# Feed-forward and expert layers: where TensorE transposes the hidden tiles, set further apart

## The chip, the cores and the metric

The kernel runs on one core of a Trainium2 chip. The metric is the device time of one execution in microseconds (us); lower is better. TensorE (PE in the profile) multiplies, VectorE (DVE) and ScalarE (ACT) read its results out of PSUM, GpSimd (POOL) helps in the first layer, SyncE (SP) issues the weight loads.

## What is computed

Two layers over 640 tokens (128 context tokens and 512 latent ones), model width 1024. Each layer has a token mixer and then a channel mixer; the change touches the channel mixers alone: a dense SwiGLU in layer 0, a top-2-of-8 expert SwiGLU in layer 1.

```python
def swiglu(h, w_gu, w_down):
    gate, up = jnp.split(h @ w_gu, 2, axis=-1)
    return (jax.nn.silu(gate) * up) @ w_down

def moe_swiglu(h, router_w, w_gu, w_down):          # D_FF_E = 1408, N_EXPERTS = 8
    probs = jax.nn.softmax((h @ router_w).astype(jnp.float32), axis=-1)
    top_p, top_i = lax.top_k(probs, TOP_K)
    ...
    for e in range(N_EXPERTS):
        y = y + gates[..., e:e + 1] * swiglu(h, w_gu[e], w_down[e])
    return y
```

The dense layer has `D_FF = 2816`, which the kernel computes as two "experts" of 1408 over all tokens.

## The kernel before

**Tiles.** Tokens go in tiles of 128. The dense layer runs its two passes over 5 tiles each. In the expert layer each expert takes its own tokens, gathered into `n` tiles, a number known only at run time; in this case the eight experts have 1, 2, 2, 1, 2, 1, 2 and 3 tiles, 14 in all.

**Precision.** Every float32 product is made of three matmuls of split operands: `hi*whi`, `lo*whi`, `hi*wlo` (lines 1261 to 1263, into one PSUM bank). `whi` is written by ScalarE (line 1988, one instruction for each half slot), `wlo` by VectorE (lines 2652 and 2661; in the dense layer every odd one by GpSimd, line 1505).

**Half slots.** Weights come in 18 slots for an expert, each of two half slots `m` of two rows of 128 (one row in two places). Gate and up take six column groups `j = 0..5` of four half slots `s = 0..3`; a group is 512 columns wide, but the last, `j = 5`, only 256. Down takes two groups of six half slots (`m = 24..35`). In each half slot (`half`, line 1247) TensorE goes over all token tiles, 6 matmuls for a tile. Four half slots of `whi` and `wlo` exist, so ScalarE splits `m + 4` once `m` has been used (`high_after`, line 1988). The SBUF ring `wring` holds three slots; SP refills one when both of its halves are split (line 504).

**The hidden tiles.** When a column group is done, ScalarE takes silu of the gate half into `hbuf` (line 2043) and VectorE multiplies the up half in (line 2686, signal `h_done`). TensorE then transposes tile `t` of `hbuf` (`h_group`, lines 1229 to 1235: two 128x128 transposes, one for `j = 5`), all into the same PSUM bank 7. ScalarE copies it to `hTh` (line 2032), VectorE writes the rest, `hTl` (line 2674, signal `hTl_ready`). Since there is one bank, `h_group` of a tile waits at line 1232 until the `hTl` of the tile before is written. So the transposes of a column group form a chain PE, ACT, DVE, PE, tile by tile.

**Where they stand.** The transposes of group `j - 1` are issued in the second half slot (`s = 1`) of group `j`, that of tile `t` right behind the matmuls of tile `t` (`after`, lines 1329 and 1330); those of `j = 5` stand in the same way in half slot 1 of the down product (line 1350). In the expert layer each further tile sits in a nested `If` on `n` (`nest`, line 1237).

**What sets the order.** Each engine's program is written out by hand and runs in order. On ScalarE it is, for each `j`: `high_after(4j)`, then `h_high` (a loop over the `n` tiles that waits for each tile's transposes), `high_after(4j+1)`, `high_after(4j+2)`, the silus, `high_after(4j+3)`. VectorE: `low` of the half slot 4j+4, `h_low` over the `n` tiles, `odd_low` (4j+5), `low` (4j+6), products, `odd_low` (4j+7). At the end of `j = 1` of an expert ScalarE also issues the loads of the next expert's tokens (line 2019), one for each tile, ahead of the splits of `j = 2`.

Of the kernel before, what the change touches and what calls it, by code (L numbers as in the profile page):

```python
# [151 lines left out]
def backbone(nc, A, out_prompt, out_sample, out_state, mod_dram, xs_dram, ys_dram, xpark, combo_dram):  # L152
    with ExitStack() as ctx:
# [565 lines left out]
        def _(pe):  # L719
# [29 lines left out]
            for k in range(KD):  # L749
                s = slot(k)  # L750
# [465 lines left out]
            def ffn(l):  # L1216
# [12 lines left out]
                def h_group(q, j, t):  # L1229

                    pe.wait_ge(f["h_done"], q + 1)
                    pe.wait_ge(f["hTl_ready"], q + 1)
                    for c in range(2 if j < 5 else 1):
                        mm = pe.transpose(bank(7)[:, c * P:(c + 1) * P], hbuf[:, t, c * P:(c + 1) * P], ident)  # L1234
                    mm.then_inc(f["hT_ps"], 1)

                def nest(n, body, t=0):

                    body(t)
                    if t + 1 < T:  # L1240
                        if isinstance(n, int):
                            nest(n, body, t + 1)
                        else:
                            with pe.If(n > t + 1):
                                nest(n, body, t + 1)

                def half(e, m, n, hi, lo, c0, bk, first, last, done, width, free, after=None):

                    k, s = m // 2, m % 2
                    nk = half_rows(k, s)  # L1250
                    pe.wait_ge(slot_split[s], split_count(k, e, l))
                    hs = (2 * ring0 + m) % HALVES

                    def tile(t):
                        if first:
                            free(t)
                        tt = slice(t * P, (t + 1) * P)
                        for c in range(nk):
                            wh, wl = whi[:, hs, c, 0:width], wlo[:, hs, c, 0:width]
                            out = bank(bk(t))[:, 0:width]  # L1260
                            pe.matmul(out, hi[:, c0 + c, tt], wh, start=(first and c == 0), stop=False)  # L1261
                            pe.matmul(out, lo[:, c0 + c, tt], wh, start=False, stop=False)  # L1262
                            mm = pe.matmul(out, hi[:, c0 + c, tt], wl, start=False, stop=(last and c == nk - 1))  # L1263
                        mm.then_inc(done if last else f["half_done"], 1)
                        if after is not None:
                            after(t)
                    nest(n, tile)
# [36 lines left out]
                def expert(e, n, c):  # L1304

                    n2 = T
                    if l:
                        pe.wait_ge(f["xTl_ready"], (c + n) * 2 + 1)
                    for j in range(6):
                        bk = (lambda t, j=j: t if j % 2 == 0 or t > 1 else 5 + t)  # L1310
                        def free(t, j=j):
                            if l == 0 and c == 0 and j == 0:
                                pe.wait_ge(f["xTl_ready"], 2 * (t + 1) + 1)
                            if t < 2 and j < 2:


                                if j:
                                    pe.wait_ge(f["y_copied"], c * 2 + 1)
                            elif j == 0 and l == 0:
                                pe.wait_ge(f["y_copied"], c + t + 2 if c else 1)  # L1320
                            elif j == 0:
                                pe.wait_ge(f["y_copied"], c * 2 + 1)
                            else:
                                pe.wait_ge(f["h_done"], c * 6 + n * (j - 1 if t > 1 else j - 2) + (t + 1))
                        for s in range(4):
                            after = None
                            if l == 0 and e == 0 and j == 0 and s == 0:
                                after = lambda t: h_columns(T - 2 + t) if t < 2 else None
                            if s == 1 and j:
                                after = lambda t, j=j: h_group(c * 6 + n * (j - 1) + t, j - 1, t)  # L1330
                            half(e, 4 * j + s, n, xTh, xTl, 2 * s, bk, s == 0, s == 3, f["gu_ps"],
                                 512 if j < 5 else 256, free, after)
                            if l and j == 1 and s == 0:
                                n2 = next_count(pe, e)

                    if l:
                        pe.wait_ge(f["xs_in"], (c + n + n2) * 16)
                    for a in range(2):
                        bk = (lambda t, a=a: t if a == 0 or t > 1 else 5 + t)
                        free = (lambda t: pe.wait_ge(f["y_copied"], c * 2 + (t + 2))) if a else \  # L1340
                            (lambda t: pe.wait_ge(f["h_done"], c * 6 + n * 5 + (t + 1)) if t > 1 else None)
                        for s in range(6):
                            m = 6 * a + s
                            if l == 0 and e and m >= 9:
                                if m == 9:
                                    last_halves((33, 34, 35), bk, f["down_ps"])
                                continue
                            if a == 0 and s == 0:
                                pe.wait_ge(f["hTl_ready"], c * 6 + n * 5 + 1)
                            after = (lambda t: h_group(c * 6 + n * 5 + t, 5, t)) if m == 1 else None  # L1350
                            half(e, 24 + m, n, hTh, hTl, 2 * s, bk, s == 0, s == 5, f["down_ps"], 512,
                                 free if a == 0 else (lambda t: free(t) if t > 1 else None), after)
                            if m == (3 if l else 2):

                                pe.wait_ge(f["hTl_ready"], c * 6 + n * 6 + 1)
                            if m == 4 and l:

                                pe.wait_ge(f["xTl_ready"], 2 * (c + n) + 2)
                            if m == 11:

                                pe.wait_ge(f["y_copied"], c * 2 + n + 1)
                            if m >= 2 and l:
                                t2, g = (m - 2) // 2, m % 2
                                if t2 == 0:
                                    xs_group(c + n, t2, g, xs_bank(m), 1)
                                else:
                                    with pe.If(n2 > t2):
                                        xs_group(c + n, t2, g, xs_bank(m), 1 if m == 4 else 0)
                    return n2
# [1655 lines left out]
```

## Time and profile before

| | us |
|---|---|
| median of 3 runs | 2067.35 |
| lowest, highest | 2066.21, 2075.73 |
| span of the profiled execution | 2066.3 |
| TensorE busy in it | 1925.3 (93%) |
| VectorE busy | 1120.1 (54%) |
| ScalarE busy | 749.5 (36%) |
| waits of the `hbuf` transposes for `hTl` | 13.6, in 16 places |

The profiled execution lies 1.05 us under the median. The feed-forward layer stands from about 740 to 1200 us of the span, the experts from about 1282 to 2017 us. "Busy" of TensorE is the time in which a matmul is in flight; matmuls overlap, so small delays between them don't show as idle time. They are read from the starts: in these stretches a 512-column matmul starts 0.227 us after the one before, a 256-column one 0.118 us after.

### The profile page before, as it was taken

To read this page: it belongs to the slowest core of one execution; us is meant where nothing else is said; L and a number is where in the kernel's file an instruction comes from. 1 tells how busy PE (TensorE), PEld (TensorE's weight loads), DVE (VectorE), ACT (ScalarE), POOL (GpSimd) and SP (SyncE) were. 2 spreads that over 40 slices of the span, in tenths; PEclk is the share of its full clock that TensorE was granted. 3 is DMA by queue.
4 is the path that set the end of the run, shared out by engine and by line. 5 is a ranking of instruction groups with operands and counts; after the bars stand their busy time and mean duration, and the time that the engine had idled before them with its cause. 6 is when DMAs were issued, how large, how long until landed. Compare 5 with 4: busy or idle time off the path is not lost. (4 is left out here: it accounts for less than half of the span.)

```text
span 2066.3 us, 39450 instructions
## 1 busy us (share of the span) xinstructions
PE 1925.3 (93%) x14595; PEld 1556.4 (75%) x14596; DVE 1120.1 (54%) x1756; ACT 749.5 (36%) x1292; POOL 407.6 (20%) x316
## 2 busy tenths in 40 slices
PE   5899999999999999999999997899998998899994
PEld 3888888888875487887888776777776786777781
DVE  3566777677674734232222385754558457554337
ACT  2523442443231122221222113744457447443332
POOL 0244344434421222121121333000000000000003
PEclk7899999999999999999999999999999999999997
DMA  8143234224326342243323506966569569654354
GB/s 298 32 146 97 91 116 137 80 93 141 116 77 213 109 143 78 93 152 99 98 92 105 174 21 246 312 216 193 181 211 317 190 198 328 217 176 164 101 174 168
DMA packets 186858, 320.03 MB, mean 155 GB/s; under 512 B 26137, under 2 KB 77729, under 8 KB 186619
## 3 DMA queue, kind: packets, MB, share of 16 engines
q1 hardware_dynamic: 170683, 286.00, 42.2%
q10 hardware_dynamic: 12192, 17.00, 2.4%
q0 software_dynamic: 3744, 13.63, 1.8%
q8 instruction: 175, 2.87, 0.6%
q14 instruction: 64, 0.52, 0.1%
HBM read 283.89 MB, written 32.67 MB: 153 GB/s over the span
## 5 line engine op out<-in xcount | busy, mean ns | idle before, releaser
L1261 PE MATMUL pp<-whi,xTh 128*128 128x512 f32 (+1 forms) x1152 | 445.5, 387 | 23.9 <-issue 8.8
L1988 ACT ACTIVATE whi<-wring 128x1024 fp32r<-128x1024 f32 (+1 forms) x324 | 314.7, 979 | 410.7 <-PE pp L1263 353.9
L1263 PE MATMUL pp<-wlo,xTh 128*128 128x512 f32 (+1 forms) x1152 | 432.4, 375 | 0.0
L1262 PE MATMUL pp<-whi,xTl 128*128 128x512 f32 (+1 forms) x1152 | 431.7, 375 | 0.0
L2652 DVE TENSOR_TENSOR wlo<-wring,whi 128x1024 fp32r<-128x1024 f32 (+1 forms) x180 | 209.6, 1164 | 269.8 <-ACT whi L1988 221.8
L1261 PEld LDWEIGHTS pp<-whi,xTh 128*128 128x128 f32 x1152 | 219.1, 190 | 74.0 <-issue 28.7
L1263 PEld LDWEIGHTS pp<-wlo,xTh 128*128 128x128 f32 x1152 | 218.8, 190 | 39.2
L1262 PEld LDWEIGHTS pp<-whi,xTl 128*128 128x128 f32 x1152 | 219.6, 191 | 34.6
L1261 PE MATMUL pp<-whi,hTh 128*128 128x512 f32 x503 | 202.3, 402 | 7.7 <-DVE ybuf L2604 2.3
L1263 PE MATMUL pp<-wlo,hTh 128*128 128x512 f32 x503 | 196.5, 391 | 0.0
L1262 PE MATMUL pp<-whi,hTl 128*128 128x512 f32 x503 | 196.1, 390 | 0.0
L2661 DVE TENSOR_TENSOR wlo<-wring,whi 128x1024 fp32r<-128x1024 f32 (+1 forms) x144 | 159.1, 1105 | 65.8 <-ACT whi L1988 55.1
L1505 POOL TENSOR_TENSOR wlo<-wring,whi 128x1024 fp32r<-128x1024 f32 (+1 forms) x38 | 97.4, 2565 | 373.7 <-ACT whi L1988 348.5
L1675 POOL DMA_INDIRECT yA<-expert_out,pos x5 | 4.7, 947 | 746.4 <-POOLq L1671 745.2
L2674 DVE TENSOR_TENSOR hTl<-pp,hTh 128x256 f32 (+1 forms) x144 | 57.7, 401 | 165.3 <-ACT hTh L2032 165.3
L2686 DVE TENSOR_TENSOR hbuf<-hbuf,pp 128x256 f32<-128x256 f32 (+1 forms) x144 | 56.6, 397 | 145.6 <-ACT hbuf L2043 145.6
L1543 POOL TENSOR_TENSOR x<-x,cmd 128x320 f32<-128x320 f32 x96 | 94.7, 1004 | 183.0 <-DVE x L2311 96.9
L1838 ACT ACTIVATE x<-pp 128x320 f32<-128x320 f32 (+1 forms) x96 | 37.6, 435 | 232.2 <-PE pp L914 232.0
L1261 PEld LDWEIGHTS pp<-whi,hTh 128*128 128x128 f32 x503 | 94.5, 188 | 31.8 <-DVE ybuf L2604 4.5
L1263 PEld LDWEIGHTS pp<-wlo,hTh 128*128 128x128 f32 x503 | 94.4, 188 | 20.5
L1262 PEld LDWEIGHTS pp<-whi,hTl 128*128 128x128 f32 x503 | 94.7, 188 | 17.5
L2032 ACT ACTIVATE hTh<-pp 128x256 f32 (+1 forms) x144 | 52.6, 365 | 137.8 <-PE pp L1234 137.7
(331 smaller groups left out, 3128.6 us busy)
## 6 DMA issues: line engine op xcount, KB each, us to landing
wring<-in_moe_w_gu SPq DMA_DIRECT2D x320, 256.0 KB, 3.8
wring<-in_ada_w SPq DMA_DIRECT2D x80, 512.0 KB, 4.7
wring<-in_moe_w_down SPq DMA_DIRECT2D x160, 256.0 KB, 3.7
wring<-in_ffn_w_gu SPq DMA_DIRECT2D x80, 256.0 KB, 3.0
wring<-in_dn_w_in SPq DMA_DIRECT2D x128, 128.0 KB, 2.7
wring<-in_ffn_w_down SPq DMA_DIRECT2D x40, 256.0 KB, 3.0
expert_in<-zeros SPq DMA_DIRECT2D x36, 256.0 KB, 3.3
wring<-in_ada_w SPq DMA_DIRECT2D x32, 256.0 KB, 5.5
```

The costliest lines, as they stand in the source:

```text
L1261: pe.matmul(out, hi[:, c0 + c, tt], wh, start=(first and c == 0), stop=False)
L1262: pe.matmul(out, lo[:, c0 + c, tt], wh, start=False, stop=False)
L1263: mm = pe.matmul(out, hi[:, c0 + c, tt], wl, start=False, stop=(last and c == nk - 1))
L1505: pool.tensor_tensor(wlo[:, hs, 0:nk, 0:w], wring[:, ring_p.slot(k), 2:2 + nk, 0:w], whi[:, hs, 0:nk, 0:w].bitcast(F32), ALU.subtract).the ...
L1543: pool.tensor_tensor(per_block(offd[:, d, :]), per_block(adiag[:, d, :]), diag_bc(LEVEL + lv, d), ALU.mult)\
L1838: act.activation(vt[rows_of, d, :], PP[d][rows_of, 0:NC], ACT.Copy).then_inc(S["vt_sb"], 1)
L1988: act.activation(whi[:, hs, 0:nk, 0:w], wring[:, ring_v.slot(k), 2 * s:2 * s + nk, 0:w], ACT.Copy)\
L2032: act.activation(hTh[:, 2 * j:2 * j + nk, bass.ds(t * P, P)], bank(7)[:, 0:nk * P].rearrange("p (k t) -> p k t", k=nk), ACT.Copy)\
L2652: dve.tensor_tensor(wlo[:, hs, :, 0:w], wring[:, ring_v.slot(k), 0:2, 0:w], whi[:, hs, :, 0:w].bitcast(F32), ALU.subtract).then_inc(slot_s ...
L2661: dve.tensor_tensor(wlo[:, hs, 0:nk, 0:w], wring[:, ring_v.slot(k), 2:2 + nk, 0:w], whi[:, hs, 0:nk, 0:w].bitcast(F32), ALU.subtract).then ...
L2674: dve.tensor_tensor(hTl[:, 2 * j:2 * j + nk, bass.ds(t * P, P)], bank(7)[:, 0:nk * P].rearrange("p (k t) -> p k t", k=nk), hTh[:, 2 * j:2 ...
L2686: dve.tensor_tensor(hbuf[:, t, 0:w], hbuf[:, t, 0:w], bank(b)[:, w:2 * w], ALU.mult)\
```

## The change

Only the places of `h_group` in TensorE's program move. `half` gets a second hook, `ahead(t)`, called ahead of tile `t`'s matmuls; `after(t)` stays behind them.

- Dense layer, `j = 5` (256 columns): the transposes stand behind tiles 0, 2 and 4 of half slot 1 and behind tiles 1 and 3 of half slot 2, two tiles' matmuls apart instead of one. The other groups of the dense layer are as they were.
- Experts, every group and the down product: tile 0's transposes stay behind tile 0 in half slot 1; those of tile `t >= 1` stand ahead of tile `t`'s matmuls in half slot 2. An expert with one tile is as it was.

```diff
+                def h_groups(q0, j, s, short):
+
+                    def group(t):
+                        h_group(q0 + t, j, t)
+                    if l:
+                        return (lambda t: group(t) if t == 0 else None) if s == 1 else None, \
+                            (lambda t: group(t) if t else None) if s == 2 else None
+                    if short:
+                        return lambda t: group(t // 2 if s == 1 else 3 + t // 2) if t % 2 == s - 1 else None, None
+                    return group if s == 1 else None, None
+
...
-                def half(e, m, n, hi, lo, c0, bk, first, last, done, width, free, after=None):
+                def half(e, m, n, hi, lo, c0, bk, first, last, done, width, free, after=None, ahead=None):
...
+                        if ahead is not None:
+                            ahead(t)
...
-                            if s == 1 and j:
-                                after = lambda t, j=j: h_group(c * 6 + n * (j - 1) + t, j - 1, t)
+                            ahead = None
+                            if s in (1, 2) and j:
+                                after, ahead = h_groups(c * 6 + n * (j - 1), j - 1, s, j == 5)
...
-                            after = (lambda t: h_group(c * 6 + n * 5 + t, 5, t)) if m == 1 else None
+                            after, ahead = h_groups(c * 6 + n * 5, 5, m, False) if m in (1, 2) else (None, None)
```

TensorE's program, dense layer, first pass, `j = 5`, half slot 1, from tile 0's transposes to tile 1's. `hTl_ready0` and `h_done0` are the dense layer's signals. Before:

```order
L1234 MATMUL pp<-cm,hbuf 128x128 [waits hTl_ready0,h_done0]
L1234 MATMUL pp<-cm,hbuf 128x128
L1261 MATMUL pp<-whi,xTh 128x256
L1262 MATMUL pp<-whi,xTl 128x256
L1263 MATMUL pp<-wlo,xTh 128x256
L1261 MATMUL pp<-whi,xTh 128x256
L1262 MATMUL pp<-whi,xTl 128x256
L1263 MATMUL pp<-wlo,xTh 128x256
L1234 MATMUL pp<-cm,hbuf 128x128 [waits hTl_ready0,h_done0]
```

Now, from tile 2's transposes, which end half slot 1, on to where tile 3's stand in half slot 2 (the product's lines are 1274 to 1276 here):

```order
L1234 MATMUL pp<-cm,hbuf 128x128 [waits hTl_ready0,h_done0]
L1234 MATMUL pp<-cm,hbuf 128x128
L1274 MATMUL pp<-whi,xTh 128x256 [waits slot_split_first]
L1275 MATMUL pp<-whi,xTl 128x256
L1276 MATMUL pp<-wlo,xTh 128x256
...
L1276 MATMUL pp<-wlo,xTh 128x256
L1234 MATMUL pp<-cm,hbuf 128x128 [waits hTl_ready0,h_done0]
```

Between two transposes with their waits there were 6 matmuls; there are 12 now.

TensorE's program, expert layer, `j = 1`: `slot_split_first` is the wait with which a half slot begins, the branches are the nested `If`s. Before, in half slot 1, tile 0's transposes, tile 1's matmuls, tile 1's transposes:

```order
L1231 ISA
L1234 MATMUL pp<-cm,hbuf 128x128 [waits hTl_ready1,h_done1]
L1234 MATMUL pp<-cm,hbuf 128x128
L1244 COMPARE_AND_BRANCH
L1261 MATMUL pp<-whi,xTh 128x512
L1262 MATMUL pp<-whi,xTl 128x512
L1263 MATMUL pp<-wlo,xTh 128x512
L1261 MATMUL pp<-whi,xTh 128x512
L1262 MATMUL pp<-whi,xTl 128x512
L1263 MATMUL pp<-wlo,xTh 128x512
L1231 REGISTER_ALU
L1234 MATMUL pp<-cm,hbuf 128x128 [waits hTl_ready1,h_done1]
```

Now, the start of half slot 2, where tile 1's transposes stand:

```order
L1255 UNCONDITIONAL_BRANCH
L1262 REGISTER_ALU
L1274 MATMUL pp<-whi,xTh 128x512 [waits slot_split_first]
L1275 MATMUL pp<-whi,xTl 128x512
L1276 MATMUL pp<-wlo,xTh 128x512
L1274 MATMUL pp<-whi,xTh 128x512
L1275 MATMUL pp<-whi,xTl 128x512
L1276 MATMUL pp<-wlo,xTh 128x512
L1255 COMPARE_AND_BRANCH
L1231 REGISTER_ALU
L1234 MATMUL pp<-cm,hbuf 128x128 [waits hTl_ready1,h_done1]
L1234 MATMUL pp<-cm,hbuf 128x128
```

Tile 1's transposes have moved from the end of half slot 1, behind one tile's matmuls, to behind tile 0 of half slot 2: with two tiles they stand 12 matmuls behind tile 0's transposes instead of 6, and no longer right ahead of a change of half slot. The programs of the other engines are unchanged.

## Rows read from the trace of the kernel before

**Rows 1.** The page: shares of the chain that ended last, by engine.

```profile
PE 28%; DVE 3%; issue 2%; DMA 2%; ACT 2%; SPq 1%; ACTq 0%; another core or an unknown queue 0%; DVEq 0%; POOL 0%; POOLq 0%
```

**Rows 2.** What the transposes of `hbuf` (line 1234) waited for: us, times.

```profile
  DVE hTl L2674: 13.6, 16
```

**Rows 3.** Timeline, dense layer, j = 5: start, duration, engine, line [idle before].

```profile
870.45 0.41 PE L1234 MATMUL pp<-cm,hbuf 128*128 128x128 f32 x2 [0.55 <-DVE hTl L2674]
...
872.12 0.41 PE L1234 MATMUL pp<-cm,hbuf 128*128 128x128 f32 x2 [0.55 <-DVE hTl L2674]
```

**Rows 4.** Timelines of ScalarE and VectorE over the same tile.

```profile
870.99 0.38 ACT L2032 ACTIVATE hTh<-pp 128x256 f32 x1 [1.29 <-PE pp L1234]
...
871.55 0.42 DVE L2674 TENSOR_TENSOR hTl<-pp,hTh 128x256 f32 x1 [1.25 <-ACT hTh L2032]
```

**Rows 5.** Timeline of TensorE, dense layer, j = 4 (512 columns), two tiles' transposes.

```profile
845.58 0.41 PE L1234 MATMUL pp<-cm,hbuf 128*128 128x128 f32 x2
...
847.25 0.41 PE L1234 MATMUL pp<-cm,hbuf 128*128 128x128 f32 x2
```

**Rows 6.** Timelines of TensorE, third expert (two tiles), 512 columns wide.

```profile
1459.64 0.40 PE L1263 MATMUL pp<-wlo,xTh 128*128 128x512 f32 x1
...
1460.65 0.39 PE L1262 MATMUL pp<-whi,xTl 128*128 128x512 f32 x1
...
1481.53 0.39 PE L1263 MATMUL pp<-wlo,xTh 128*128 128x512 f32 x1
...
1482.21 0.39 PE L1262 MATMUL pp<-whi,xTl 128*128 128x512 f32 x1
...
1486.55 0.39 PE L1263 MATMUL pp<-wlo,xTh 128*128 128x512 f32 x1
1486.78 0.39 PE L1261 MATMUL pp<-whi,xTh 128*128 128x512 f32 x1
...
1514.79 0.40 PE L1263 MATMUL pp<-wlo,hTh 128*128 128x512 f32 x1
...
1515.75 0.39 PE L1262 MATMUL pp<-whi,hTl 128*128 128x512 f32 x1
```

**Rows 7.** The same expert, j = 5 (256 columns), timeline of TensorE.

```profile
1503.56 0.38 PE L1234 MATMUL pp<-cm,hbuf 128*128 128x128 f32 x2
...
1504.37 0.28 PE L1263 MATMUL pp<-wlo,xTh 128*128 128x256 f32 x1
1505.92 0.41 PE L1234 MATMUL pp<-cm,hbuf 128*128 128x128 f32 x2 [1.26 <-DVE hTl L2674]
...
1506.66 0.28 PE L1262 MATMUL pp<-whi,xTl 128*128 128x256 f32 x1
```

**Rows 8.** Timeline of TensorE, seventh expert (two tiles), j = 2.

```profile
1791.15 0.38 PE L1234 MATMUL pp<-cm,hbuf 128*128 128x128 f32 x2
...
1794.71 0.41 PE L1234 MATMUL pp<-cm,hbuf 128*128 128x128 f32 x2 [1.79 <-DVE hTl L2674]
```

**Rows 9.** Timeline of TensorE, last expert (three tiles), j = 5.

```profile
1960.40 0.41 PE L1234 MATMUL pp<-cm,hbuf 128*128 128x128 f32 x2 [1.27 <-DVE hTl L2674]
...
1962.07 0.66 PE L1234 MATMUL pp<-cm,hbuf 128*128 128x128 f32 x2 [0.55 <-DVE hTl L2674]
```

**Rows 10.** Windows: length, busy (count) of PE, PEld, DVE, ACT, POOL; clock; DMA share; GB/s.

```profile
1453.00:1533.00 80.00, 77.18 (x367) 62.61 (x368) 44.88 (x58) 39.74 (x59) 0.00 (x0) 1.00 0.60 189
1535.00:1592.00 57.00, 50.29 (x234) 38.76 (x233) 42.93 (x49) 38.37 (x52) 0.00 (x0) 1.00 0.91 311
...
1960.00:1965.00 5.00, 4.05 (x22) 3.77 (x23) 1.83 (x4) 1.76 (x3) 0.00 (x0) 0.70 0.39 128
```

**Rows 11.** Timeline of VectorE, third expert: the split behind `j = 3`'s transposes.

```profile
1485.37 1.22 DVE L2661 TENSOR_TENSOR wlo<-wring,whi 128x1024 fp32r<-128x1024 f32 x1 [0.45 <-ACT whi L1988]
```

**Rows 12.** The chain that ended last, in the fourth expert (one tile).

```profile
1545.35 1.07 ACT whi L1988
...
1556.16 8.60 DMA wring<-in_moe_w_gu
```

More of the change, by code:

```diff
@@ L1328, in expert @@
                                 after = lambda t: h_columns(T - 2 + t) if t < 2 else None
-                            if s == 1 and j:
-                                after = lambda t, j=j: h_group(c * 6 + n * (j - 1) + t, j - 1, t)
+                            ahead = None
+                            if s in (1, 2) and j:
+                                after, ahead = h_groups(c * 6 + n * (j - 1), j - 1, s, j == 5)
                             half(e, 4 * j + s, n, xTh, xTl, 2 * s, bk, s == 0, s == 3, f["gu_ps"],
-                                 512 if j < 5 else 256, free, after)
+                                 512 if j < 5 else 256, free, after, ahead)
                             if l and j == 1 and s == 0:
@@ L1349, in expert @@
                                 pe.wait_ge(f["hTl_ready"], c * 6 + n * 5 + 1)
-                            after = (lambda t: h_group(c * 6 + n * 5 + t, 5, t)) if m == 1 else None
+                            after, ahead = h_groups(c * 6 + n * 5, 5, m, False) if m in (1, 2) else (None, None)
                             half(e, 24 + m, n, hTh, hTl, 2 * s, bk, s == 0, s == 5, f["down_ps"], 512,
-                                 free if a == 0 else (lambda t: free(t) if t > 1 else None), after)
+                                 free if a == 0 else (lambda t: free(t) if t > 1 else None), after, ahead)
                             if m == (3 if l else 2):
```

## Prediction

> **What bounds the kernel now.** I read the page first: by the table above TensorE is busy for 93% of the span, ScalarE for 36% and VectorE for 54%, and TensorE holds by far the largest named share of the chain that ended last [rows 1]. So the question is where TensorE loses time at the instructions that the change moves. The view of what line 1234 waits for gives it: 13.6 us in 16 places, all for `hTl` [rows 2]. The timelines place them: 4 in each pass of the dense layer at 0.55 us (4.4) [rows 3], one in each of the four two-tile experts at `j = 5` at 1.26 us (5.0) [rows 7], two in the last expert, 1.27 and 0.55 us (1.8) [rows 9], one of 1.79 us in the seventh expert [rows 8], and what remains of the 13.6, 0.6 us, in the second expert at `j = 2`.
>
> What ends these waits is the chain through bank 7. From the start of a tile's transposes at 870.45, ScalarE starts 0.54 us later and takes 0.38, VectorE starts at 1.10 and ends at 1.52 [rows 4], and the next transposes start at 1.67 us [rows 3]. With 512 columns the same spacing stands in the trace, 1.67 us, but without idle time [rows 5]: one tile's 6 matmuls (1.36 us) and the transposes' own time fill it. With 256 columns 6 matmuls are only 0.71 us.
>
> Idle time is not all. I take as the cost of a group of transposes the time from the last matmul ahead of it to the second one behind it, less two matmuls. Tile 0's group, for which nothing has to be waited, costs 1482.21 - 1481.53 - 0.45 = 0.23 us; tile 1's, at the end of the half slot, costs 1460.65 - 1459.64 - 0.45 = 0.55 us at `j = 1` and 1515.75 - 1514.79 - 0.45 = 0.51 us in the down product [rows 6]. Of the five such places in a two-tile expert these are the first and the last; the three between them cost 0.60, 0.67 and 0.74. A change of half slot without transposes costs nothing: 1486.55 to 1486.78 is one matmul [rows 6]. So the extra arises where TensorE's sequencer has just been held by the wait for `hTl` and then has the branches of the nested `If` and the next half slot's wait ahead of it with nothing queued.
>
> **Dense layer, j = 5.** Two tiles of 256 columns (12 x 0.118 = 1.42 us) and a group's 0.23 make 1.65 us between transposes, against the 1.67 us that the chain needs. The transposes keep their spacing, but each of the four gaps in a pass now holds one tile's matmuls more, 0.71 us: 8 x 0.71 = **5.7 us**. The first and the last transposes keep their times, so ScalarE and VectorE, which run in order behind them, are no later on the clock; only TensorE is earlier, by 2.8 us a pass. The next thing that could be late is the split of half slot 24. It follows the last `hTl` and ends some 2.7 us after the last transposes start (1.10 + 0.42 + 1.22, a split's time from rows 11), and TensorE needs it after one more tile and one half slot of 256 columns (6 x 0.71 = 4.2 us). Cover is 1.5 us, so I cost it at nothing; were the split 2.8 us later than read, a pass would give back 1.3 us.
>
> **Two-tile experts, 512 columns and down.** Tile 1's transposes now stand 12 matmuls behind tile 0's: 0.23 + 12 x 0.227 = 2.95 us, against 1.67 us for the chain. The wait is over 1.3 us before TensorE gets there, so the sequencer stays ahead, and the group should cost what tile 0's costs. The five places cost 0.55 + 0.60 + 0.67 + 0.74 + 0.51 = 3.07 us, and would cost 4 x 0.23 + 0.12 = 1.04 (the down group has one transpose, 0.12 for tile 0): 2.03 us for an expert, four experts **8.1 us**. At the least the end-of-half part stays, at the most the groups cost as said.
>
> **Two odd places.** In the seventh expert ScalarE is still busy with the token loads, and the chain takes 3.56 us [rows 8]; with 2.95 us of cover 0.6 of the 1.79 us wait stays: 1.1 us more than the ordinary place, and 0.75 at the 0.6 us wait of the second expert: **1.9 us**.
>
> **Two-tile experts, j = 5.** VectorE splits a half slot first, so the chain takes 2.36 us; cost now 1506.66 - 1504.37 - 0.24 = 2.05 us [rows 7]. Matmuls cover 0.23 + 12 x 0.118 = 1.65 us; 0.71 us of wait stays, and the group, behind a wait again, costs 0.31 on top (1.67 - 1.36, rows 5). That would save 1.03. Behind it only one 0.71 us tile stands ahead of the next change of half slot, and I charge 0.25 us for it (0.55 - 0.31): 0.8 us, four times **3.2 us**; between 2.2 (the wait alone) and 4.1.
>
> **Last expert.** Three tiles: tile 1's group gets three tiles of cover, tile 2's keeps one. At 512 columns tile 2's end-of-half cost goes (0.3 at each of four places), tile 1's 0.06 each, down 0.3; at `j = 5` the wait of 1.27 us goes with its group's slack (1.45), the second, 0.55 us, stays but moves off the half slot's end (0.4): **3.6 us**. There the clock also fell: behind these two waits the window of 5 us shows a mean granted clock of 0.70 [rows 10], that is 3 us at 1.2 instead of 2.4 GHz, which costs 1.5 us. With the first wait gone I take **1.3 us** of it as saved; it could be none.
>
> **Sum.** 5.7 + 8.1 + 1.9 + 3.2 + 3.6 + 1.3 = 23.8 us off a span of 2066.3: 2042.5. The profiled execution lies 1.05 us under the median, so 2043.6 for the median. What no edit touches: one-tile experts, three of eight.
>
> **Rival 1: the end-of-half cost stays (2051.3).** If the 0.3 us is the price of the half slot's change beside any group, or comes back in half slot 2, only the waits go. Lost are 0.24 + 0.29 + 0.36 + 0.43 + 0.3 = 1.6 us in four experts and 1.2 in the last, 7.7 us. Against it: changes of half slot without transposes cost nothing [rows 6]. The Trainium skill (Advanced Engine Details and Errata, section Control Flow Timing) puts a compare-and-branch at about 108 ns; by that 21 places would give 2.3 of the 7.7 us and the time would be about 2049. The trace shows more than that for one place, and the rows decide for me.
>
> **Rival 2: given back in the one-tile experts (2053).** There the DMA engines are busy for 0.91 of the time at 311 GB/s, against 0.60 and 189 GB/s with two tiles [rows 10], and the chain runs through an 8.6 us load [rows 12]. If weights set the clock of the whole stretch, the gains of the second, third and fifth experts, about 9.5 us, end as longer waits in the fourth and sixth. Against it: the load starts when a ring slot is free, and the chain leads from it back to a ScalarE split at 1545.35 that waited for TensorE [rows 12]. A TensorE that comes earlier frees it earlier.
>
> **Rival 3: slower (2078).** ScalarE runs in order. In `h_high` it now waits for tile 1's transposes a tile longer (1.36 us), and behind that wait stand the splits of half slots 4j+5 and 4j+6, on VectorE their `wlo`, on SP the loads into the slots that these free. If TensorE had to wait for them, 25 places at up to 1.4 us would cost 35 us, 11 more than is saved. It decides once the slack of that split is under 1.4 us. In the third expert it ended at 1485.37 + 1.22 = 1486.6 [rows 11] and was needed 24 matmuls after 1486.78, at 1492.2: slack 5.6 us. The loads into the freed slots start up to 1.4 us later too; with the DMA engines busy for 0.60 of the time they have room [rows 10]. The Trainium skill (TensorE: Matmul & The Clock Gate, section on the array as 16x 32x32) says that ScalarE and VectorE are strict FIFO with 8 entries; by that rule the held splits can't pass the wait. No row here shows a split that passed one.
>
> **How the numbers follow.** Forecast 0.77 (own range 2040 to 2048: upper ends of the bounded terms above, down to the clock's gain lost, `j = 5` at its lower end and the dense cover partly gone), rival 1 0.10, rival 2 0.07, rival 3 0.04, the rest for what I don't see. The range 2040 to 2054 takes in the first two rivals. About 0.5% (10 us) is what a measurement of this kernel can tell from no change; the first three cases all lie beyond it. Faster 0.91, same 0.05, slower 0.04.
>
> **What would show it.** Right: the waits of line 1234 for `hTl` fall from 13.6 us to about 4.5 (four of 0.7, 0.6, 0.55 and little else); the dense `j = 5` transposes stay 1.67 us apart without idle; tile 1's group in experts costs 0.23 us; two-tile experts shorten by some 3 us each, one-tile experts stay. Wrong: waits of line 1274 for `wlo` in two-tile experts (rival 3), longer one-tile experts (rival 2), costs of 0.5 us at the change from half slot 1 to 2 or 2 to 3 (rival 1), or a clock that falls at another place.

## The result, and the profile after

| | before, beside it | changed |
|---|---|---|
| median of 4 runs, us | 2069.5 | 2044.72 |
| lowest to highest | 2066.21 to 2075.73 | 2039.09 to 2045.42 |
| span of the profiled execution | 2066.3 | 2043.6 |
| TensorE busy in it | 1925.3 | 1915.1 |

The ratio is 0.987, with a 95% interval of 0.9855 to 0.9886. The forecast was 2043.6 us, the stated range 2040 to 2054.

In the changed kernel line 1261 has become 1274 (`hi*whi`), 1262 is 1275, 1263 is 1276; `hTl` is written at line 2688, `hTh` at 2046, `hbuf` at 2057 and 2700, `whi` at 2002, `wlo` at 2666 and 2675. The transposes are still issued at line 1234. The view of what line 1234 waited for, of the changed kernel (us in total, times), answers to [rows 2]:

```profile
  DVE hTl L2688: 3.2, 6
```

The waits for `hTl` fell from 13.6 us in 16 places to 3.2 in 6; about 4.5 had been forecast.

**Dense layer, j = 5.** The timeline of TensorE (start us, us, engine, line, operation) at the same two groups as in [rows 3]:

```profile
869.86 0.28 PE L1276 MATMUL pp<-wlo,xTh 128*128 128x256 f32 x1
869.98 0.41 PE L1234 MATMUL pp<-cm,hbuf 128*128 128x128 f32 x2
...
871.54 0.28 PE L1276 MATMUL pp<-wlo,xTh 128*128 128x256 f32 x1
871.66 0.40 PE L1234 MATMUL pp<-cm,hbuf 128*128 128x128 f32 x2
```

The transposes stand 1.68 us apart, as before (1.67), but the last matmul now starts 0.12 us ahead of them and no idle time is printed: two tiles' matmuls fill the gap that held one.

**Third expert.** TensorE around tile 1's group at 512 columns, and at `j = 5`; these answer to [rows 6] and [rows 7]:

```profile
1464.49 0.39 PE L1276 MATMUL pp<-wlo,xTh 128*128 128x512 f32 x1
1464.72 0.38 PE L1234 MATMUL pp<-cm,hbuf 128*128 128x128 f32 x2
1464.86 0.48 PE L1274 MATMUL pp<-whi,xTh 128*128 128x512 f32 x1
1465.17 0.39 PE L1275 MATMUL pp<-whi,xTl 128*128 128x512 f32 x1
...
1495.51 0.28 PE L1276 MATMUL pp<-wlo,xTh 128*128 128x256 f32 x1
1496.34 0.41 PE L1234 MATMUL pp<-cm,hbuf 128*128 128x128 f32 x2 [0.55 <-DVE hTl L2688]
1496.50 0.36 PE L1274 MATMUL pp<-whi,xTh 128*128 128x256 f32 x1
1496.70 0.28 PE L1275 MATMUL pp<-whi,xTl 128*128 128x256 f32 x1
```

By the prediction's measure the group costs 1465.17 - 1464.49 - 0.45 = 0.23 us, what tile 0's costs, against 0.55 to 0.74. At `j = 5` a wait of 0.55 us is left and the group costs 1496.70 - 1495.51 - 0.24 = 0.95 us, against 2.05.

Whether the wait for `hTl` has held the sequencer can be read from VectorE's timeline. These are tile 0's `hTl` in the kernel before and in the changed one, in the third expert:

```profile
1459.35 0.42 DVE L2674 TENSOR_TENSOR hTl<-pp,hTh 128x256 f32 x1
```

```profile
1462.90 0.42 DVE L2688 TENSOR_TENSOR hTl<-pp,hTh 128x256 f32 x1
```

Before, it ended at 1459.77, and tile 1's transposes started 0.15 us later, at 1459.92: they were held, though no idle time is printed. Now it ends at 1463.32, 1.40 us ahead of the transposes at 1464.72. Below, "held" or "bound by the chain" means such a start 0.15 us behind the `hTl`.

**Where the 22.7 us of the span went.** For the whole layers I use stretches between the starts of tile 0's transposes, which the change leaves in place: "j = 1 to 5" runs from tile 0's transposes in group `j = 1` to those in `j = 5`, "j = 5 to down" from there to those in the down product. All are differences of two start times in the trace.

| stretch, us | before | changed | difference |
|---|---|---|---|
| start to the dense layer's first transposes | | | -0.5 |
| the two dense passes | 373.05 | 367.24 | -5.8 |
| dense layer to first expert | 161.65 | 163.32 | +1.7 |
| first expert (1 tile) | 62.96 | 63.12 | +0.2 |
| second expert's j = 1 to the last expert's down | 618.27 | 599.29 | -19.0 |
| from there to the end | 92.62 | 93.39 | +0.8 |

The last stretch holds the down groups of the last expert, which cost 0.28 us less than before; the rest of it is 1.05 us longer.

Within the experts ("whole" is from tile 0's transposes at `j = 1` to those at the next expert's `j = 1`):

| expert (tiles), stretch | before | changed |
|---|---|---|
| second (2), j = 1 to 5 | 46.10 | 43.61 |
| third (2), j = 1 to 5 | 45.29 | 43.61 |
| fifth (2), j = 1 to 5 | 45.23 | 43.61 |
| seventh (2), j = 1 to 5 | 47.08 | 44.25 |
| the four, j = 5 to down | 9.83 to 9.99 | 8.86 to 8.87 |
| fourth (1), whole | 68.46 | 68.80 |
| sixth (1), whole | 67.98 | 67.23 |
| last (3), j = 1 to 5 | 67.55 | 66.03 |
| last (3), j = 5 to down | 15.61 | 12.61 |

### The profile page after: what moved, and what is told of

Its sections match the earlier page's. It is cut to its first block and busy times, and to the rows that moved or that the text cites. A ratio compares the mean times of both kernels' runs of the same rounds, so it can differ in the third digit from the quotient of the medians.

```text
span 2043.6 us, 39450 instructions
## 1 busy us (share of the span) xinstructions
PE 1915.1 (94%) x14595; PEld 1554.2 (76%) x14596; DVE 1118.8 (55%) x1756; ACT 746.3 (37%) x1292; POOL 407.5 (20%) x316
```

## The experiments

The theory is the prediction's: two tiles' matmuls between transposes let the chain through bank 7 run beside them; and a group of transposes costs more than its own 0.23 us only where TensorE's sequencer has been held by the wait and meets the end of a half slot at once. The rivals are that the end of a half slot costs the 0.3 us by itself, that the one-tile experts give the gain back, and that a held ScalarE makes the splits late.

The kernels of experiments 1 and 2 and the first of 3 were measured beside one measurement of the kernel before (median 2064.5 us), the second of 3 and those of 4 and 5 beside another (2068.32); experiment 6 is a single execution beside a single one (2070.22). Ratios are to be compared within one of the groups; the stretches of the experts with two and three tiles repeat closely in all traces, those of the one-tile experts do not.

**1. The dense part alone, and the experts' part alone.** In the first, the expert layer keeps its places:

```diff
                     if l:
-                        return (lambda t: group(t) if t == 0 else None) if s == 1 else None, \
-                            (lambda t: group(t) if t else None) if s == 2 else None
+                        return group if s == 1 else None, None
```

> Only the dense layer's j = 5 transposes are set apart; the experts' stand as before. The theory (each of eight gaps of 1.67 us holds one tile of 256 columns more) expects 5.7 us less than before, a span near 2060.5, with the experts' 13.6 - 4.4 = 9.2 us of waits for hTl kept. If the saved time were given back in the pool stage or the experts, the span would stay within 2 us of before.

The second leaves out `if short:` and its `return`, so the dense layer keeps its places.

> Only the experts' transposes of tiles 1 and up move to half slot 2; the dense layer is as before. The theory expects 17 to 18 us less than before, a span near 2048.5, and the two parts to add up: 5.7 + 17.5 = 23 us. If the parts overlapped (a common limit such as the weight loads), their sum would be clearly over the 22.7 us that both together took off the span.

Measured: 2056.74 us, ratio 0.9962 (0.9946 to 0.9978), and 2048.03 us, ratio 0.992 (0.9897 to 0.9943). What line 1234 waited for, first in the kernel with the dense part alone, then in the one with the experts' part alone:

```profile
  DVE hTl L2687: 9.2, 8
```

```profile
  DVE hTl L2686: 7.6, 14
```

The dense passes take 367.21 us with the dense part alone and 373.02 with the experts' alone; the stretch from the second expert's `j = 1` to the last one's down product takes 614.01 and 598.18. So each part acts in its own layer, and the two add up to the change's stretches (367.24, 599.29). The sum of the two ratios' gains, 0.4% and 0.8%, is near the whole 1.3%. The dense part's is 7.8 us of median with a wide interval, against 5.8 in its stretch. For the experts' part 17 to 18 us were expected; its stretch gave 20.1 and its median 16.5.

**2. Tile 1's transposes two half slots' matmuls behind tile 0's, but at the end of a half slot again.** In the experts they stand behind tile `t` of half slot 2 instead of ahead of it:

```diff
-                        return (lambda t: group(t) if t == 0 else None) if s == 1 else None, \
-                            (lambda t: group(t) if t else None) if s == 2 else None
+                        return (lambda t: group(t) if t == 0 else None) if s == 1 else \
+                            (lambda t: group(t) if t else None), None
```

> As the changed kernel, but in the experts tile t's transposes stand behind tile t's matmuls in half slot 2, so tile 1's of a two-tile expert again end a half slot, now 18 matmuls behind tile 0's and long after the wait is over. If the 0.3 to 0.5 us of an end-of-half group came from a sequencer held by the wait, the group costs 0.23 us here too, and the 0.7 us wait at j = 5 goes: about 3 us less than the changed kernel, a span near 2040.5. If it came from the place at the end of a half slot, 21 places cost 0.3 to 0.4 us more each: about 4 us more than the changed kernel, near 2048.

Measured: 2039.81 us, ratio 0.9885 (0.9861 to 0.9908). TensorE's timeline of this kernel, at the end of a half slot in the third expert (two tiles, no wait for `hTl`), and at the same place of the last expert (tile 2 of three, where the chain has only one tile of cover):

```profile
1471.13 0.39 PE L1276 MATMUL pp<-wlo,xTh 128*128 128x512 f32 x1
1471.36 0.38 PE L1234 MATMUL pp<-cm,hbuf 128*128 128x128 f32 x2
1471.49 0.48 PE L1274 MATMUL pp<-whi,xTh 128*128 128x512 f32 x1
1471.81 0.39 PE L1275 MATMUL pp<-whi,xTl 128*128 128x512 f32 x1
...
1887.16 0.40 PE L1276 MATMUL pp<-wlo,xTh 128*128 128x512 f32 x1
1887.44 0.41 PE L1234 MATMUL pp<-cm,hbuf 128*128 128x128 f32 x2
1887.87 0.50 PE L1274 MATMUL pp<-whi,xTh 128*128 128x512 f32 x1
1888.21 0.40 PE L1275 MATMUL pp<-whi,xTl 128*128 128x512 f32 x1
```

The first group costs 1471.81 - 1471.13 - 0.45 = 0.23 us, the second 1888.21 - 1887.16 - 0.45 = 0.60. Both are followed by the same change of half slot and branches; only the second was bound by the chain. The last expert's four such groups cost 0.52 to 0.60. In the changed kernel tile 2's group is chain-bound too, but stands in mid half slot, and costs 0.29 to 0.31. So rival 1 falls: the 0.3 us belongs to neither the wait nor the end of the half slot alone, but to both together. The dense layer fits: its chain-bound groups in the last tile of a half slot, where there is no `If`, cost 0.27 to 0.30 at 512 columns.

The trace of the kernel before has the same comparison in its one-tile experts, whose groups all stand at the end of half slot 1 and have no tile ahead of them to wait for. In the first expert, `j = 2` and `j = 3` (TensorE), and the product into `hbuf` ahead of the second (VectorE):

```profile
1297.89 0.39 PE L1263 MATMUL pp<-wlo,xTh 128*128 128x512 f32 x1
...
1298.57 0.39 PE L1262 MATMUL pp<-whi,xTl 128*128 128x512 f32 x1
...
1304.31 0.41 DVE L2686 TENSOR_TENSOR hbuf<-hbuf,pp 128x256 f32<-128x256 f32 x1
1304.56 0.39 PE L1263 MATMUL pp<-wlo,xTh 128*128 128x512 f32 x1
1304.78 0.44 PE L1234 MATMUL pp<-cm,hbuf 128*128 128x128 f32 x2
...
1305.71 0.39 PE L1262 MATMUL pp<-whi,xTl 128*128 128x512 f32 x1
```

At `j = 2` the product had been ready for over 1 us, and the group cost 1298.57 - 1297.89 - 0.45 = 0.23 us. At `j = 3` it ended at 1304.72, 0.06 us ahead of the transposes, and the group cost 1305.71 - 1304.56 - 0.45 = 0.70 us, though the split of the next half slot had been written by 1304.4. The other one-tile experts give the same: 0.23 us at `j` = 1 and 2, 0.67 to 0.71 at `j` = 3 and 4, where the product comes 0.06 to 0.10 us ahead. It is the same half slot's end in all of them, and the same `If`. This fits a wait for the product that holds the sequencer as the wait for `hTl` does.

There is a gain on top: at `j = 5` the group meets no wait any more (0.5 us in 1 place are left in the whole kernel, against 3.2 in 6), and the four stretches "j = 5 to down" take 8.30 us instead of 8.87. In the seventh expert the odd wait at `j = 2` goes too (43.61 instead of 44.25). In the last expert "j = 1 to 5" grows from 66.03 to 67.08, since tile 2's groups are back at the half slot's end, and "j = 5 to down" from 12.61 to 12.76. That is 4 x 0.57 + 0.64 - 1.05 - 0.15 = 1.7 us less than the change, where about 3 were expected; by the ratios (0.9885 here, 0.9870 and 0.9883 for the change, each in its own group) no difference shows.

**3. How much later may tile 1's transposes come?** In these two the transposes that stood in half slot 2 of `j = 1` to `4` stand in half slot 3, ahead of tile `t` in one and behind it in the other:

```diff
-                            (lambda t: group(t) if t else None) if s == 2 else None
+                            (lambda t: group(t) if t else None) if s == (3 if j < 4 else 2) else None
...
-                            if s in (1, 2) and j:
+                            if s and j:
```

> As the changed kernel, but in the experts' 512-column groups tile 1's and later transposes stand another half slot later (half slot 3), so ScalarE is held for 4.3 us instead of 1.4 ahead of two splits. With the slack of 5.6 us that was read for the first of them nothing should be late by more than some tenths: 0 to 3 us more than the changed kernel, a span of 2043.5 to 2046.5. If the held splits were what TensorE waits for already, each of 20 places would cost up to 2.7 us: over 30 us more, with waits for wlo ahead of the product's matmuls.

```diff
-                        return (lambda t: group(t) if t == 0 else None) if s == 1 else None, \
-                            (lambda t: group(t) if t else None) if s == 2 else None
+                        return (lambda t: group(t) if t == 0 else None) if s == 1 else \
+                            (lambda t: group(t) if t else None) if s == 3 and j < 4 else None, \
+                            (lambda t: group(t) if t else None) if s == 2 and j > 3 else None
...
-                            if s in (1, 2) and j:
+                            if s and j:
```

> As the kernel with half slot 3, but behind tile t instead of ahead of it: ScalarE is held 5.7 us instead of 4.3. The slack read for the held split of half slot 4j+5 is 5.6 us, so this should be past the point from which the order on ScalarE decides: in two-tile experts some 0.3 to 1 us more at each of 16 places, and more in the last expert, 8 to 20 us more than the changed kernel, with waits for wlo or for the products (hbuf) ahead of matmuls. If the time stays within 2 us of the changed kernel, the slack is larger than I read it and the rival that forecast slower was further off than stated.

Measured: 2044.75 us, ratio 0.9917 (0.9885 to 0.9948) for the first, in one group with the 0.9885 of experiment 2; 2064.83 us, ratio 0.9975 (0.9962 to 0.9989) for the second, in one group with the change's 0.9883.

| | before | changed | ahead in half slot 3 | behind in half slot 3 |
|---|---|---|---|---|
| third expert, tile 0's to tile 1's transposes, j = 1 | 1.65 | 2.98 | 5.69 | 7.05 |
| third expert, j = 1 to 5 | 45.29 | 43.61 | 43.61 | 45.64 |
| last expert, j = 1 to 5 | 67.55 | 66.03 | 70.36 | 77.41 |

A chain that goes on 4.0 us longer than before costs the third expert nothing (the other two-tile ones take 43.61 to 43.68 us); one that goes on 5.4 us longer costs it 2.0 us over the change, 0.4 from one `j` to the next up to `j = 4` and 0.8 from there to `j = 5` (the others take 45.63 to 45.66), and 0.2 more from `j = 5` to down. The slack that the prediction read in the third expert was 5.6 us. The place of the cost, in the timelines of VectorE and of TensorE of the kernel with the transposes behind tile `t` in half slot 3 (its lines are one higher):

```profile
1464.21 0.42 DVE L2689 TENSOR_TENSOR hTl<-pp,hTh 128x256 f32 x1 [6.62 <-ACT hTh L2047]
1465.08 1.22 DVE L2676 TENSOR_TENSOR wlo<-wring,whi 128x1024 fp32r<-128x1024 f32 x1 [0.44 <-ACT whi L2003]
...
1465.88 0.39 PE L1277 MATMUL pp<-wlo,xTh 128*128 128x512 f32 x1
1466.36 0.50 PE L1275 MATMUL pp<-whi,xTh 128*128 128x512 f32 x1
```

VectorE waits 6.62 us for tile 1, then for ScalarE's split, and its own split ends at 1465.08 + 1.22 = 1466.30; TensorE, with matmuls 0.227 us apart, is 0.25 us late at 1466.36. By this lateness the slack here is about 5.15 us, an estimate from 5.4 - 0.25. That is rival 3's mechanism, in the place that it named. The change's own extra distance is 1.3 us.

In the last expert it sets in earlier, and through another engine's work: with the transposes ahead in half slot 3 the stretch grows by 4.3 us over the change, more than the 0 to 3 us expected for the whole kernel. What TensorE waited for from 1860 to 1960 us, in that kernel:

```profile
PE pp L1274 <- DVE hbuf L2700: 3.2, 4, 0.8
```

Here the next group's products (`hbuf`, VectorE) stand behind tile 2's `hTl`, and it is the PSUM bank that they free which comes late, at all four places. The waits of line 1274 for `wlo` sum to 11.2 us in 12 places here and to 5.9 in 8 in the changed kernel, but that is no sign of the edit: most of them stand in the one-tile experts, and the change's second trace has 7.5 and the trace of the experts' part alone 10.5. With the transposes behind tile `t` in half slot 3 this stretch grows by 11.4 us, and the clock falls in it (mean granted clock 0.98 over 77.41 us, which is 3.1 us at 1.2 GHz). Its median is 18.4 us over the change's, within the 8 to 20 expected.

**4. The change again, and only the transposes at j = 5 moved to the end of half slot 2.** The second of these keeps the change and puts this ahead of it:

```diff
+                    if l and j == 4:
+                        return (lambda t: group(t) if t == 0 else None) if s == 1 else \
+                            (lambda t: group(t) if t else None), None
                     if l:
```

> The changed kernel once more, beside the others of this call: 1.3% less time than before (22 to 24 us). Its stretch from the first two-tile expert's first transposes to the last expert's down product took 599.3 us in its first profile against 618.3 us before; the theory expects that within 1.5 us, whatever the rest of the span does.

> As the changed kernel, but the transposes that the experts' j = 5 hosts stand behind tile t in half slot 2. The theory: 0.96 us falls to 0.4 us at one place in each of four two-tile experts and the last expert keeps its 512-column places at 0.29 us instead of 0.5 to 0.6, so 2.3 us less than the changed kernel in the experts' stretch, a ratio to the changed kernel of 0.999. If the later hTl makes the down product wait at its start, the 2.3 us come back as waits there.

Measured: 2046.47 us, ratio 0.9883 (0.9857 to 0.9908) for the change, 2042.05 us, ratio 0.9864 (0.9838 to 0.989) for the other. The change's long stretch took 597.1 us, 2.2 less than in its first trace, where no more than 1.5 had been expected: the fourth expert, with one tile, took 66.7 us instead of 68.8, and the experts with two and three tiles repeated within 0.1 us from their `j = 1` to their down product. In the other kernel the four stretches "j = 5 to down" take 8.30 or 8.31 us against 8.86 to 8.88 in the change, and the other stretches of the experts with more than one tile repeat within 0.1 us, but for the last expert's "j = 5 to down", 12.83 against 12.61. That is 4 x 0.57 - 0.2 = 2.1 us: the version that keeps the good places of both. The intervals of the two ratios overlap, so the gain over the change is shown by the stretches, not by the medians.

**5. VectorE writes `hTl` before its split at j = 5.** The change, with only the order of VectorE's program changed in the group whose chain is longest:

```diff
-                        if l:
+                        if l and j < 5:
                             low(2 * j + 2, e)
...
+                        if l and j == 5:
+                            low(2 * j + 2, e)
```

> As the changed kernel, but in the experts' j = 5 VectorE writes the hTl ahead of the split of half slot 24. If that split is what makes the chain 2.36 us instead of 1.67, the 0.7 us wait at j = 5 goes (0.96 to 0.25 us a place), and the split, now behind tile 1's hTl, is late at the start of the down product by about 0.4 us: 0 to 2 us less than the changed kernel. If the wait stays, the split was not its cause.

Measured: 2044.92 us, ratio 0.9878 (0.9852 to 0.9903). Tile 1's transposes at `j = 5` now follow tile 0's after 1.65 us instead of 2.36, so the split was what made this chain long, and their group costs 0.24 to 0.25 instead of 0.95 us; but "j = 5 to down" only fell from 8.87 to 8.57. TensorE at the start of the third expert's down product in this kernel:

```profile
1497.11 0.28 PE L1276 MATMUL pp<-wlo,xTh 128*128 128x256 f32 x1
1497.53 0.50 PE L1274 MATMUL pp<-whi,hTh 128*128 128x512 f32 x1
1497.86 0.40 PE L1275 MATMUL pp<-whi,hTl 128*128 128x512 f32 x1
```

The first matmul of the down product starts 0.42 us behind the last of `j = 5`, where in the changed kernel it starts 0.12 us behind (1498.62 and 1498.74), and the next one 0.33 instead of 0.23. So of the 0.7 us, 0.4 came back at the wait for the split that now stands behind `hTl`. The waits of line 1274 for `wlo` sum to 12.7 us in 15 places, against 5.9 in 8, but only three of the new ones, 0.16 us each, stand at this place (the second, fifth and seventh experts); nearly all the rest is in the one-tile experts, where the order of VectorE's program changed too. Moving TensorE's transposes (experiment 4) frees the same chain without making a split late, and is worth 0.57 in the same stretch.

**6. The kernel before, again.** No edit.

> The kernel before once more, unchanged. If the two waits of the last expert at j = 5 are what brought the clock down there, the clock falls again at that place and the stretch from its j = 5 transposes to its down product takes 15.6 us. If the fall was chance (the kernel with the dense part alone has the same two waits, kept its clock and took 14.3 us), it is missing here and the stretch takes 14.3 us. Two-tile experts should repeat 45.2 to 45.3 and 10.0 us.

Measured: 2071.59 us, span 2069.8, waits of line 1234 for `hTl` 13.7 us in 16 places. The dense passes and the second, third and fifth experts' stretches repeat within 0.15 us; the one-tile experts' differ by 0.8 to 2.2. In the seventh expert "j = 1 to 5" took 48.70 instead of 47.08, and in the last "j = 5 to down" 14.31 instead of 15.61. The windows over the two places, of this trace (columns: busy time and instructions of PE, PEld, DVE, ACT and POOL, granted clock as a share of full speed, DMA share, GB/s):

```profile
1795.00:1805.00 10.00, 8.20 (x30) 6.15 (x29) 4.01 (x5) 4.15 (x6) 0.00 (x0) 0.83 0.85 281
1950.00:1980.00 30.00, 28.06 (x160) 23.75 (x159) 12.59 (x21) 11.33 (x21) 0.00 (x0) 1.00 0.41 130
```

In this run the clock fell to its lower level behind the 1.79 us wait of the seventh expert, and not behind the two in the last expert, where it had fallen in the first trace [rows 10]. With the dense part alone it fell at neither place (14.31 us in the last expert). This gives the fall a price: 15.61 - 14.31 = 1.30 us.

## Why the prediction was right

| step | forecast | measured |
|---|---|---|
| dense j = 5 | 5.7 | 5.8 |
| two-tile experts, j = 1 to 5 and down, ordinary places | 8.1 | 7.8 |
| the two odd places | 1.9 | 2.0 |
| two-tile experts, j = 5 | 3.2 | 4.3 |
| last expert and its clock | 4.9 | 4.8 |
| sum of these | 23.8 | 24.7 |
| given back outside, net | 0 | 2.0 |

The time itself, 1.1 us beside the forecast, is in part luck: a gain 0.9 us larger than forecast met 2.0 us given back, 1.3 us of the gain belong to a fall of the clock that another trace of the kernel before does not have at that place, and the kernel before had a median of 2069.5 us beside the change, not the 2067.35 from which the forecast starts. The mechanism does not rest on it; the stretches show it part by part.

**The dense part** held in both halves. The passes shorten by 8 x 0.73 us, the spacing stays (1.68), and the split of half slot 24 took nothing back.

**The end of the half slot** held. A place with 512 columns gives 0.23 for its 0.55 to 0.74, an ordinary expert 1.62 to 1.68 us for 1.64 in `j = 1` to `4`, and the down product 0.37 to 0.42 for 0.39 in three experts. In the second its group costs 0.13 instead of 0.51 us too, but the stretch behind it is no shorter; in other traces with the same places there it varies by 0.7 us. Experiment 2 shows why: where the wait is over, the end of a half slot costs nothing extra. The Trainium skill's price for a compare-and-branch of about 108 ns (Advanced Engine Details and Errata, section Control Flow Timing) names the kind of thing that lies there; here a held group at a half slot's end cost 0.25 to 0.45 us more than one in mid half slot (0.54 to 0.74 in the third and fifth experts against 0.29 to 0.31), and a group there without the held wait paid none of it. That branches are what the 0.3 us consists of was argued, and is not shown: the runs show that it takes the held wait and the half slot's end together, and it was seen in the expert layer alone, with its nested `If`. Why it grows from 0.54 or 0.55 at `j = 1` to 0.74 at `j = 4` in both of these experts no run shows. The prediction's sentence on this price does not add up either: with 2.3 us for branches that stay, the time would be 2043.6 + 2.3 = 2045.9 us; the 2049 it gives holds if the branches go and the rest stays.

**The odd places** held: in the seventh expert a wait of 0.44 us is left, where 0.6 had been read, and the stretch "j = 1 to 5" gives 2.83 us; in the second it gives 2.49. Over an ordinary expert's 1.65 that is 1.2 and 0.8.

**The step that was mis-sized** is `j = 5` of the two-tile experts: 0.8 us forecast, 1.10 measured (9.97 to 8.87). The group's own cost fell as worked out, to 0.95 us from 2.05, with 0.55 of wait against 0.71 read. But I charged 0.25 us for a change of half slot one 256-column tile behind the group. It cost nothing: from the second matmul behind the group on, across the change of half slot, the starts stay 0.12 us apart, so after one tile TensorE's sequencer is ahead again. The upper end of my bounds, 4.1 for the four experts, was the sum without that charge; they gave 4.3, a little beyond it, since 0.55 us of wait stayed where 0.71 was read. The second expert gave 0.96 of it, the others 1.10 to 1.12.

**The last expert** gave 1.52 us in `j` = 1 to 5, 3.00 in `j` = 5 to down, with the clock, and 0.28 at the groups of the down product, for 1.44, 3.15 and 0.3. Of the 3.00, 1.30 is the clock's, by the kernels in which it did not fall there, which is the forecast's 1.3. But it belongs to the one profiled execution: of the three traces in which the experts' transposes stand at the old places, only this one has the fall there.

**Rival 2** fell with the one-tile experts: the fourth and sixth took 66.7 to 68.8 us in the two traces of the changed kernel, 67.2 to 70.1 in the two of the kernel before. This fits a TensorE that came earlier, freed its ring slots earlier and had its weights earlier; the loads' own times were not compared. **Rival 3** fell for this change, and experiment 3 showed both that the mechanism exists and that the slack read from the trace was its deciding point, near enough: nothing at 4.0 us, 0.4 us and more a place at 5.4, where 5.6 had been read. What that slack did not say is that in a three-tile expert something else is nearer, the bank that the products free.

**What was missed** are 2.0 us given back outside the moved places, and this is why a larger gain than forecast ended at the time forecast: 1.7 between the dense layer and the experts, 0.2 in the first expert, 1.05 at the end, less 0.5 at the start and 0.4 in the fourth and sixth experts. At the end the mean granted clock was 0.83 over the changed kernel's last 93.4 us and 0.86 over the 92.6 of the kernel before; that this is the 1.05 us is not shown. Most of the 1.7 is one stretch. The windows from the first to the second group of small matmuls behind the dense layer (line 1412 before, 1426 in the changed kernel), of the kernel before and of the changed one:

```profile
1205.07:1214.10 9.03, 9.03 (x36) 6.71 (x36) 8.39 (x9) 0.00 (x0) 2.72 (x2) 0.81 0.01 2
```

```profile
1198.76:1209.44 10.68, 10.68 (x37) 7.44 (x37) 9.35 (x10) 0.00 (x0) 2.72 (x2) 0.68 0.01 2
```

The same work (the second window takes in the start of the next group's first matmul, hence x37, and of one VectorE instruction that had not begun in the first), 1.65 us longer, with a mean granted clock of 0.68 instead of 0.81: 6.8 us at 1.2 GHz instead of 3.4. The stretch is 10.68 us in seven of the eight traces with the dense part of the change, and 9.03 or 9.04 in the three without it (before, before again, the experts' part alone). The eighth, the kernel with the transposes behind tile `t` in half slot 3, has the same program for the dense layer and this stage, and shows 8.99 us at 0.81. So it goes with the dense change, but does not follow from it each time. What moves the clock's return stays open: the work of that stretch and the wait ahead of it (1.33 us for `ybuf`) are the same in the kernel before and the changed one.

## What to carry to other kernels

A wait that a chain of engines causes is worth more than its idle time if, as at the end of a half slot here, branches and another wait stand right behind it in the waiting engine's program: move the instruction one piece of work further on, and count both. How far it may go is the slack of whatever the helping engines have queued behind it, read for each shape apart, because the nearest follower is not the same with two tiles as with three. When a chain is shortened, move the consumer rather than reorder the helping engine: the reordering made a split late and gave 0.30 us where the move gave 0.57.

## What was not expected of the hardware

- The cost of a held wait at the end of a half slot: a group of transposes took 0.23 us there when the sequencer was ahead and 0.52 to 0.60 when it was held, by the same instructions (experiment 2), and 0.23 against 0.70 in one expert of the kernel before.
- The clock's fall is not tied to one place: in two traces of the same kernel it fell to 1.2 GHz behind a wait at 1962 us in one and behind one at 1798 us in the other. A third trace with the experts' transposes at their old places has neither fall. Of the eight traces in which they are moved, seven show a mean granted clock of 1.00 over the seventh and the last expert's gate and up; the eighth, whose last expert has new waits of up to 1.9 us (experiment 3), 0.98; the other kernel of experiment 3, with new waits of up to 0.8 us there, shows 1.00. That the waits cause the falls is suggested by this and not shown.
- The same stage took 10.68 us or 9.03 behind the dense layer, by how long the clock stayed at 1.2 GHz (6.8 or 3.4 us), with the same work in it.
- Some waits belong to the run and not to the kernel: the one for the first expert's tokens was 5.0 us in the changed kernel's first trace, 5.5 in its second and 1.5 in that of the dense part alone. With the long wait the clock fell too (mean 0.77 over 1270 to 1285 us, against 1.00 with the short one), and the stretch ahead of the experts took 163.3 us instead of 157.3. Spans of different runs are therefore no measure for an edit of a few microseconds; stretches of the trace are.
